# Output turning of two attention layers dealt between the chunks of the next weight block, in a float32 block stack on one core

## The reference, cut to what matters

```python
for l in range(2):
    shift, scale, gate = split(silu(c) @ w_ada[l] + b_ada[l], 3)
    h  = rms(x, norm_w[l]) * (1 + scale) + shift          # and hc for the context
    ...                                                   # h @ w_in[l], three attentions, z
    y = concat(o_a, o_b, o_c) * silu(z)
    x = x + gate * (y @ w_out[l])                         # and xc for the context when l == 0
```

## Time and profile before

| | |
|---|---|
| runs | 3939.87, 3941.35, 3943.05 us; median 3941.35 |
| profiled execution | 3936.85 us; its span 3934.9 us, 1.95 us less |
| TensorE matmul busy | 3663.5 us of the span |
| VectorE, ScalarE busy | 2009.1 us, 1669.7 us |
| mean granted TensorE clock | 0.967 of full speed |
| all traffic | 577.48 MB, mean 147 GB/s |

### The profile page before, as it was taken

The page is one execution under the profiler, slowest core; times in us unless marked ns, Lnnn a source line. Parts: engine busy times, 40 slices in busy tenths (PEclk is TensorE's granted clock), DMA queues, the critical chain, the costliest instruction groups (busy, mean ns, idle before and its releaser), DMA issues.

```text
span 3934.9 us, 46177 instructions
## 1 busy us (share of the span) xinstructions
PE 3663.5 (93%) x18672; PEld 2947.6 (75%) x18672; DVE 2009.1 (51%) x3102; ACT 1669.7 (42%) x2653; POOL 68.1 (2%) x118
## 2 busy tenths in 40 slices
PE   7899999999899899999898999999999699999997
PEld 1677777878777677777776777766777599999776
DVE  1665654344666656543354544445455366666444
ACT  2323344433411434455535434454355455545333
POOL 1200000000020000000000000000000000000000
PEclk8999999999999899999999999999999899999999
DMA  9643321233274454324364566535645256666554
GB/s 361 191 140 114 97 60 54 60 105 103 92 218 153 131 188 145 86 64 114 90 204 141 161 178 178 156 112 169 186 142 173 86 161 187 184 187 187 182 187 145
DMA packets 350740, 577.48 MB, mean 147 GB/s; under 512 B 25268, under 2 KB 131012, under 8 KB 348352
## 3 DMA queue, kind: packets, MB, share of 16 engines
q1 hardware_dynamic: 344208, 549.47, 45.2%
q0 software_dynamic: 6320, 25.06, 2.3%
HBM read 570.26 MB, written 4.19 MB: 146 GB/s over the span
## 4 chain that ended last, share of the span: by engine, by line
PE 55%; DVE 5%; ACT 3%; DMA 2%; issue 1%; SPq 0%; ACTq 0%; DVEq 0%
PE ps L696 35%; PE ps L1542 13%; DVE w_lo L665 2%; PE ps L1265 1%; DMA raw_ring<-in_w_in_dram 1%; ACT w_hi L659 1%; PE ps L1177 1%; PE ps L1435 1%; PE ps L1442 1%; PE ps L1150 1%; PE ps L1159 0%; PE ps L732 0%; DVE r_a L2183 0%; PE ps L1069 0%; ACT f_arena L1588 0%
## 5 line engine op out<-in xcount | busy, mean ns | idle before, releaser
L665 DVE TENSOR_TENSOR w_lo<-raw_ring,w_hi 128x1024 fp32r<-128x1024 f32 (+1 forms) x827 | 1006.6, 1223 | 1177.1 <-ACT w_hi L659 1176.1
L659 ACT CAST w_hi<-raw_ring 128x1024 fp32r<-128x1024 f32 (+1 forms) x827 | 861.4, 1048 | 1274.2 <-PE ps L696 544.7
L696 PE MATMUL ps<-w_hi,r_a 128*128 128x512 f32 x3552 | 1308.3, 408 | 58.8 <-DVE w_lo L665 21.4
L696 PE MATMUL ps<-w_lo,r_a 128*128 128x512 f32 (+1 forms) x2624 | 1041.5, 397 | 0.0
L696 PE MATMUL ps<-w_hi,r_b 128*128 128x512 f32 (+1 forms) x2272 | 860.5, 398 | 11.6 <-DVE w_lo L665 6.0
L696 PEld LDWEIGHTS ps<-w_hi,r_a 128*128 128x128 f32 x3552 | 677.0, 191 | 250.3 <-issue 70.0
L696 PEld LDWEIGHTS ps<-w_lo,r_a 128*128 128x128 f32 x2624 | 501.7, 191 | 115.3 <-issue 8.6
L696 PEld LDWEIGHTS ps<-w_hi,r_b 128*128 128x128 f32 x2272 | 434.7, 191 | 121.0 <-DVE w_lo L665 12.5
L1542 PE MATMUL ps<-r_a,w_hi 128*128 128x256 f32 x2816 | 501.2, 281 | 3.0 <-DVE w_lo L665 3.0
L1542 PEld LDWEIGHTS ps<-r_a,w_hi 128*128 128x128 f32 x2816 | 433.1, 189 | 3.2 <-issue 3.2
L1542 PE MATMUL ps<-r_a,w_lo 128*128 128x256 f32 x1408 | 396.1, 281 | 0.0
(11 more groups left out here) (316 smaller groups left out, 2932.8 us busy)
## 6 DMA issues: line engine op xcount, KB each, us to landing
raw_ring<-in_w_in_dram SPq DMA_DIRECT2D x386, 512.0 KB, 3.7
raw_ring<-in_ffn_w_up_dram SPq DMA_DIRECT2D x176, 512.0 KB, 3.6
raw_ring<-in_w_ada_dram SPq DMA_DIRECT2D x128, 512.0 KB, 3.9
raw_ring<-in_w_out_dram SPq DMA_DIRECT2D x96, 512.0 KB, 3.7
raw_ring<-in_ffn_w_down_dram SPq DMA_DIRECT2D x88, 512.0 KB, 4.3
gla_arena<-in_w_ada_dram SPq DMA_DIRECT2D x64, 512.0 KB, 9.1
raw_ring<-in_w_proj_b_dram SPq DMA_DIRECT2D x32, 512.0 KB, 3.6
raw_ring<-in_w_proj_a_dram SPq DMA_DIRECT2D x16, 512.0 KB, 3.6
```

The lines of the kernel that those rows point to most:

```text
L659: nc.scalar.copy(WH[:, ph.s_slot(i, j), 0:n], RAW[:, ph.raw_slot(i, j), 0:n]).then_inc(hi_ready, 1)
L665: nc.vector.tensor_tensor(WL[:, ph.raw_slot(i, j), 0:n], RAW[:, ph.raw_slot(i, j), 0:n], WH[:, ph.s_slot(i, j), 0:n].bitcast(F32), ALU.sub ...
L696: mm = nc.tensor.matmul(PS[:, t, a:z], X(x, k, t), W[w][:, kk * cols + a:kk * cols + z], start=(k == 0 and q == 0), stop=(c == len(js) - 1 ...
```

## The change

- y is turned four groups at a time: groups 0 to 3 before block 0 of `wout`, then four after each of chunks 0, 1 and 2. The first four wait for three blocks of z only.
- The last `w_ada` sum of `z0` moves behind chunk 3, with a place of its own for the sums of `wout` (`ACC`).
- The gates go in pairs, after chunks 3 to 6 (layer 1: 3 and 4). On ScalarE their copies stand behind the split of the chunk.
- In block 0 VectorE takes `rest(q + 2)` first, then its share of y, the diagonals, and `mods` last. Blocks 1 to 3 keep `mods` first.
- The squares of `X4` are taken by 512 columns, those of blocks 0 to 2 in the middle of the next block; a dummy root comes ahead of the last. Scaling goes by halves of 1024 columns.
- `win1`: four groups are turned ahead, two after each of chunks 0 to 5. Its first two chunks are split before the norm.

```diff
 # TensorE, win1
-                    pe.wait_ge(act_x, l + 1)
-                    pe.wait_ge(dve_x, l + 1)
+                    pe.wait_ge(act_half, 1)
+                    pe.wait_ge(dve_half, 1)
...
-                    for k in range(KT):
+                    for k in range(4):
                         group(TRN[f"h{l}"][0] + k, tr_tiles(lambda t: X4[:, t, k * P:k * P + P], 4))
...
                         pe_with_sum(pe, "win", l, b, c, WT[l][b])
+                        if l and b == 0 and c < 6:
+                            if c == 2:
+                                pe.wait_ge(act_x, l + 1)
+                                pe.wait_ge(dve_x, l + 1)
+                            for k in (2 * c + 4, 2 * c + 5):
+                                group(TRN[f"h{l}"][0] + k, tr_tiles(lambda t: X4[:, t, k * P:k * P + P], 4))
 # TensorE, wout
-                pe.wait_ge(z_used, 16 * l + 4 * T)
-                for k in range(KT):
-                    group(TRN[f"y{l}"][0] + k, tr_tiles(lambda t: U[:, t, ocol(k):ocol(k) + P], T))
+                pe.wait_ge(z_used, 16 * l + 3 * T)
+                for k in range(4):
+                    turn_y(k)
...
+                for c in range(8):
+                    pe.wait_ge(tr_free, y0 + 2 * c + 2)
+                    pe_part(pe, ph, 0, S8, c, 2, NB, x1, T, AC[f"wout{l}"][0], 0, T)
+                    if c < 3:
+                        if c == 2:
+                            pe.wait_ge(z_used, 16 * l + 4 * T)
+                        for k in range(4 * c + 4, 4 * c + 8):
+                            turn_y(k)
+                    if c == 3 and l == 0:
+                        pe.wait_ge(tr_free, y0 + KT)
+                        pe_ada_sum(pe, TURN["z0", 3, 7], ACC["z"])
+                    if 3 <= c < (7 if l == 0 else 5):
+                        gate(2 * c - 6)
+                        gate(2 * c - 5)
 # ScalarE, norm and wout
-                    act.wait_ge(acc_free, AC["win1"][0][0])
-                squares([(JUNK, X4[:, t], SS[:, t:t + 1]) for t in range(4)], ss_ready)
+                    act_hi(act, PH["win1"], 0, 0)
+                    act_hi(act, PH["win1"], 0, 1)
+                    warm_root()
+                    for t in range(4):
+                        act.wait_ge(acc_free, AC["wout0"][3][0] + t + 1)
+                        part_squares(X4[:, t, 3 * NB:D], t, 3, JUNKV, ss_ready if t == 3 else None)
...
                     split(q + 2)
+                    if b == 0 and c < 3:
+                        turned_y(range(4 * c + 4, 4 * c + 8))
+                    if b == 0 and 4 <= c < (8 if l == 0 else 6):
+                        turned_gate(2 * c - 8)
+                        turned_gate(2 * c - 7)
+                    if l == 0 and b and c == 3:
+                        act.wait_ge(acc_free, AC["wout0"][b - 1][0] + 4)
+                        for t in range(4):
+                            part_squares(X4[:, t, NB * b - NB:NB * b], t, b - 1, JUNKV)
 # VectorE, wout
-                diag(0)
-                diag(1)
                 for q in range(24, 56):
                     b, c = divmod(q - 24, 8)
-                    if b == 0 and c + 2 < ng:
-                        diag(c + 2)
...
-                    mods(f"wout{l}", b, c)
-                    rest(q + 2)
+                    if b:
+                        mods(f"wout{l}", b, c)
+                        rest(q + 2)
+                    else:
+                        rest(q + 2)
+                        if c < 3:
+                            split_y(range(4 * c + 4, 4 * c + 8))
+                        if c == 2:
+                            V.memset(ones, 1.0)
+                            dve.wait_ge(ada_free, 15 if l == 0 else 24)
+                            diag(0)
+                            diag(1)
+                        if c == 4 and l == 0:
+                            dve_ada_bias(dve, TURN["z0", 3, 7])
+                            dve.wait_ge(ada_free, 16)
+                        if 4 <= c < 3 + ng // 2:
+                            diag(2 * c - 6)
+                            diag(2 * c - 5)
+                        mods(f"wout{l}", b, c)
```

More of the change, by code:

```diff
@@ L133, in build @@
         ONE = place("one", 1)
+        WARM = place("warm", 1)
         NM = place("neg_max", 2)
@@ L1321, in _ @@
                 ph, y0 = PH[f"wout{l}"], TRN[f"y{l}"][0]
-                if l == 0:
[L1323 to L1333, removed]
+                for c in range(8):
[12 more added lines that the diff above has]
+                        gate(2 * c - 5)
+                for i in range(1, 4):
+                    for c in range(8):
+                        if l == 0:
+                            pe_with_sum(pe, "wout", 0, i, c, 4)
+                        else:
+                            pe_block_part(pe, ph, i, S8, c, 2, NB, x1, range(2), AC["wout1"][i])
+                        if l == 0 and i == 2:
+                            flip(1, c)
+                if l == 0:
                     pe_ada_sum(pe, TURN["wout0", 3, 7], ACC["wout"])
                     pe.wait_ge(ada_free, 20)
[L1336 to L1343, removed]
             pe.wait_ge(act_x, XI["h2"] + 1)
@@ L1572, in copies, with to_hi @@
                 evac(PS[:, bk(n), :]).then_inc(tr_free, 1)
-            def to_hi(name, n, dst, w, scale=None):
+            def to_hi(name, ks, dst, w, scale=None):
                 n0 = TRN[name][0]
-                for k in range(n):
+                for k in ks:
                     act.wait_ge(tr_done, n0 + k + 1)
@@ L1707, in _ @@
                     b, c = divmod(q, 8)
+                    if l and b == 0 and c < 6:
+                        split(q + 2)
+                        for k in (2 * c + 4, 2 * c + 5):
+                            copies(n0 + k, lambda b: modulate(k, b))
+                        continue
                     if l == 0 and b == 0 and 2 * c + 4 < KT:
@@ L2172, in _, with split @@
             TT = nc.vector.tensor_tensor
-            def split(name, n, dst, w, scale=None):
+            def split(name, ks, dst, w, scale=None):
                 n0, s0 = TRN[name]
-                for k in range(n):
+                for k in ks:
                     dve.wait_ge(tr_hi, s0 + k + 1)
@@ L2194, in mean, with mean_parts @@
                 mean_rinv(name, T)
+            def mean_parts(name, T, width):
+                dve.wait_ge(ss_ready, SI[name] + 1)
+                L(V.tensor_reduce(SS[:, 0:T], SSP[:, 0:T, :], AX_X, ALU.add))
+                mean_eps(name, T, width)
             def mean_eps(name, T, width):
@@ L2403, in _ @@
                     rest(q + 2)
+                    if l and b == 0 and c < 6:
+                        for k in (2 * c + 4, 2 * c + 5):
+                            split_row(k, s0 + k, (tr_free, n0 + k + 1))
                     if c == 7 and b != 2:
@@ L2674, in _ @@
                 dve_lo(dve, PH["ma"], 0, j)
-            split("ya", 8, lambda x, k: YT[:, x, k, :], 256)
+            split("ya", range(8), lambda x, k: YT[:, x, k, :], 256)
             def merge_loop(name, js, add, done=0):
@@ L2822, in _ @@
             mean("hf", 2, D)
-            split("hf", KT, lambda x, k: HT[:, x, k, :], 256, lambda k: VT[:, 80 + k:81 + k])
+            split("hf", range(KT), lambda x, k: HT[:, x, k, :], 256, lambda k: VT[:, 80 + k:81 + k])
             ph = PH["up"]
```

98 lines of the change are left out of this document (62 added, 36 removed).

## The result

| | before | after |
|---|---|---|
| runs, us | 3938.10 to 3943.05, median 3941.35 (5 runs) | 3954.69 to 3961.24, median 3956.74 (5 runs) |
| ratio of the runs, 95% interval | | 1.0037 [1.0026, 1.0048] |
| span of the profiled execution | 3934.9 us | 3954.3 us |

The change makes the kernel 15.4 us slower; the forecast was some 9 us slower, with 3936 to 3962 as its range. The profiled execution of before lies under all its timed runs, so the two spans are 19.4 us apart and not 15.4. Some 4 us of what the two traces show between them is therefore chance, and I come back to it.

A forecast was written before the change was run, and what follows sets the result against it. TensorE, in matmuls for 93% of the span, was taken as the bound, so only its pauses and half-clock work could be saved; +26.4 (layer 0) - 15.6 (norm) - 1.5 (layer 1) = +9.3, so 3950.5 us, range 3936 to 3962.

The forecast's parts named there:

- the first step: Turning y in layer 0, and the ring: block 1 of `wout0` starts 26.4 us later; bounds +20 and +30.
- The turns: Block 0 of `wout0`: seven times from the end of one `mods` to the next, 78.3 us in sum.
- Part 2, the norm: Norm between the layers: block 0 of `win1` ends 15.6 us earlier; bounds 18.5 and 11.
- Part 3, layer 1: Turning y in layer 1: block 0 of `wout1` ends 1.5 us earlier; bounds 3 and -2.
- turn 3 of part 1: Block 0 of `wout0`: loads of x and ctx ahead of the ring load add 7.4 us, making 16.1.
- The loop does not close: Rival, block 0 of `wout0`: loads run far enough ahead, TensorE sets the block; 3921.5 us, clearly faster; chance 0.11.
- the x load misses it: Rival, block 0 of `wout0`: loop closes, but turn 3's ring load lands in 3.7 us; 3943.3 us, no change; chance 0.23.
- the norm gives little: Rival, norm: clock stays at half through the first four chunks, gain only 7 us; 3959 us, slower; chance 0.10.

The follow-up runs named there:

- mods_first: The change, but in block 0 of `wout` VectorE takes `mods` ahead of `rest(c+2)` as in the kernel before; 3938.2 us, ratio 0.9991 to the kernel before.
- no_x_load: The change without the two loads of x and ctx (4 MB) after y is turned in layer 0; 3950.6 us, ratio 1.0027 to the kernel before.
- norm_alone: The kernel before with only the change's norm part; turning of y, gates and `mods` order as before; 3929.1 us, ratio 0.9971 to the kernel before.
- all_mended: The change with layer 1's y turned whole, `mods`, bias and diagonals ahead of `rest`, x and ctx loaded by 512 columns; 3926.3 us, ratio 0.9958.
- change_mended: The change, y dealt in both layers, with `mods`, bias and diagonals ahead of `rest`, x and ctx loaded by 512 columns; 3924.9 us, ratio 0.9948.

## Why the prediction was right or wrong

**The sign and the mechanism** were right, and the first step came within a microsecond: forecast 26.4, measured 25.6. The median lies 6.2 us above the forecast, but that is partly luck: between the two traces the sum of +9.3 meets 19.4, 10.1 more, and the terms below say where. The turns were forecast as 11.2, 12.5, 16.1, 10.0, 9.9, 9.9, 8.7 and came as 11.2, 13.0, 15.8, 10.7, 10.0, 10.0, 8.8. `mods_first` and `no_x_load` show both causes by taking each away. On the fixed cost of a load: the forecast set the trace's 3.7 us against the Trainium skill's 3.2 (DMA: Bandwidth & Descriptors, Anatomy of one DMA); the undisturbed turns bear out 3.7, with a load of 3.7 us at 1131.48. By 3.2 they would have been 0.5 shorter each. The page gives its fit for loads that GpSimd issues, and these are SyncE's.

**Part 2, the norm** had the right marks: transposes 8.9 us after the last matmul of `wout0` and chunk 0 another 5.2 us on, both as forecast (1298.9, 1307.8, 1313.0). It was mis-sized at both ends. I took 1338.57 as the start of chunk 0; the chain only began there. Two chunks had run before it, as the timeline of the kernel before shows:

```profile
1331.62 0.78 PE L696 MATMUL ps<-w_hi,r_a 128*128 128x512 f32 x1
```

So block 0 of `win1` ended at 1355.6 and not at 1361.4, and the gain had 5.8 us less to take. On the other side a pair of groups costs 0.87 us and not 1.2, and ScalarE and VectorE keep up but for 0.3 us ahead of the last chunk; the block ended 3.0 us sooner than forecast. Together 12.8 in place of 15.6. The prediction is also at odds with itself: its signs have the first transposes 7 us after the last matmul, its sum 8.9.

**Part 3, layer 1** had the wrong sign. Its terms add up to 1993.4 against 1993.90, 0.5 us and not the 1.5 that I took; the other 1.0, for two breaks fewer, had no number behind it. I put "-2, if the loads behind the turning now catch the ring" among the bounds and took the other value. They do catch it: the reload of x goes out when y is turned, which is now 12.8 us into block 0 (1990.40) and was 1.5 us into it (1969.43), and the half clock falls on block 1. The stretches give +2.6 us (-0.2 and +2.8) for -1.5. The same mechanism as turn 3 of part 1, which I had charged with 7.4 us in layer 0, was left out in layer 1.

**The range**, 3936 to 3962, is wider than its bounds: 20 - 18.5 - 3 is -1.5 and not -5.5, so the lower end should have been 3940. The result lies in both.

**Not in the sum** are 1.7 us in blocks 1 to 3 and 2.3 in the rest. The 1.7 are the slow start of block 2 that `norm_alone` has too: the wait ahead of it is no longer (3.4 us, 3.6 before), its first 5 us are at 0.66. Only the kernel before has no squares there, and it has one trace, so whether they play a part stays open. In the rest the change moves nothing. Between the 436th and 530th ring load (counted from 0), where all these kernels are alike, the traces took 0 to 6 us more than that of before: 3.1 in the change, 4.6 in `mods_first`, 5.0 in `all_mended`, 6.2 in `no_x_load`, none in `norm_alone`, 0.2 in `change_mended`. At the 528th load one can see it happen. TensorE is busy throughout, with the same waits around, and yet the granted clock differs; the rows are before, the change, and `mods_first`:

```profile
2363.50:2365.50 2.00, 2.00 (x10) 1.59 (x10) 0.00 (x0) 0.52 (x1) 0.00 (x0) 1.00 0.00 0
2382.60:2384.60 2.00, 2.00 (x6) 1.54 (x6) 0.00 (x0) 0.00 (x0) 0.00 (x0) 0.50 0.00 0
2370.60:2372.60 2.00, 2.00 (x6) 1.52 (x6) 0.00 (x0) 0.00 (x0) 0.00 (x0) 0.50 0.00 0
```

This place alone costs the change 1.5 us and `mods_first` 3.1, and `norm_alone` nothing. What sets off such a stretch in one execution and not in another, no run here shows.

**The rivals.** "The loop does not close" and "the x load misses it" are both out, by the trace, and so is "the norm gives little", with 12.8 us. The chance of 0.49 for slower was low for a mechanism that came out so exactly; what kept it down were the errors of parts 2 and 3, 2.8 and 4.1 us, both of which made the change look better than it is.

## What to carry to other kernels

When work is dealt into a pipelined loop, follow each ring slot once around: which instruction gives it back, and what that instruction now stands behind in its queue. If a load stands ahead of the instruction that releases the next load, the ring has become a loop, here one of five slots in which each turn costs a landing and all the work behind it. And a bulk transfer that was hidden by the pause must be dealt out together with the work that filled the pause: here the change was 15 us slower, and with the order put right and x loaded by blocks it is some 20 us faster than the kernel before. But check what is left at the end of the stretch and not only at its start: most of the 20 us are the norm's, and `norm_alone`, without any dealt y, is not parted from it by the runs.

## What the runs showed of the hardware

The x load does not share the DMA engines evenly with the ring. These are the two queues (packets, MB, share of the 16 engines) in the changed kernel from 1106 to 1108, just after the ring load of 1105.02 was issued, then from 1110 to 1112; q0 is GpSimd's, q1 the ring's:

```profile
q0 software_dynamic: 102, 0.84, 99.0%
```

```profile
q0 software_dynamic: 78, 0.64, 80.7%
q1 hardware_dynamic: 79, 0.16, 21.5%
```

For 3.4 us after its issue the ring load moves nothing, where the undisturbed one of 1131.48 has its first packet after 1.1 us; after that each queue moves as many packets as the other, 78 and 79, but GpSimd's are of 8.2 KB and the ring's of 2.0 KB, so the ring gets a fifth of the bytes. The Trainium skill (DMA: Bandwidth & Descriptors, Queues, rings and completion order) has each engine take turns between its queues by packet; the trace agrees from 1110 on, if the profile's packets are counted, and does not show it for the first microseconds. By columns of 512 the pieces of x are 1 MB at a time and their packets smaller: in `change_mended` 1.05 MB in 288 packets, and the ring load issued 4 us after them lands in 4.9 us, where it took 11.8 in `mods_first`. The pieces have landed by 1099.6, 1.8 us after the issue of that load, so there was also much less of x ahead of it. Whether the size of the pieces or that of the packets does it was not told apart.
